# GpSimd's subtraction for the low part of a weight unit in four instructions of 256 columns, not two of 512

## The reference

```python
x = x + 0.5 * swiglu(rmsnorm(x, ffn1_norm), ffn1_w_gu, ffn1_w_down)     # 1024 -> 2 x 2816 -> 1024
x = x + token_mixing(rmsnorm(x, mix_norm), w_in, ...)                   # 1024 -> 3584 -> 1024
x = x + cross_attention(rmsnorm(x, xa_norm), rmsnorm(mem, mem_norm), xa_wq, xa_wkv, xa_wo)
x = x + 0.5 * swiglu(rmsnorm(x, ffn2_norm), ffn2_w_gu, ffn2_w_down)
return rmsnorm(x, final_norm)
```

## Time and profile before

| | before |
|---|---|
| median of 3 runs | 1172.21 us (1170.49 to 1172.48) |
| the profiled execution's own time | 1170.22 us |
| its span, first to last instruction | 1168.4 us |
| TensorE busy | 1141.2 us, 98% |
| TensorE weight load | 948.6 us, 81% |
| DVE busy | 471.4 us, 40% |
| ScalarE busy | 429.2 us, 37% |
| GpSimd busy | 560.1 us, 48%, all but 0.2 in 408 instructions of line 341 |
| DMA | 113.1 MB, mean 97 GB/s |

### The profile page before, as it was taken

The page is one execution under the profiler, slowest core; times in us unless marked ns, Lnnn a source line. Parts: engine busy times, 40 slices in busy tenths (PEclk is TensorE's granted clock), DMA queues, the critical chain, the costliest instruction groups (busy, mean ns, idle before and its releaser), DMA issues.

```text
span 1168.4 us, 14941 instructions
## 1 busy us (share of the span) xinstructions
PE 1141.2 (98%) x5366; PEld 948.6 (81%) x5366; DVE 471.4 (40%) x660; ACT 429.2 (37%) x576; POOL 560.1 (48%) x412
## 2 busy tenths in 40 slices
PE   7999999999999999999999999999999999999997
PEld 4888888888888788888777888888888888888886
DVE  8332233222222568788567224455322322321112
ACT  6332232232223545554346543345223223222221
POOL 5544554555555333233435873145445445455550
PEclk9999999999999999999999999999999999999999
DMA  6323222323223221221222542123232232233312
GB/s 231 106 91 107 96 90 101 103 91 106 99 104 108 90 72 55 73 73 54 82 91 87 182 157 71 53 72 109 90 108 90 90 108 90 90 108 108 108 55 72
DMA packets 33317, 113.10 MB, mean 97 GB/s; under 512 B 3712, under 2 KB 5888, under 8 KB 33152
## 3 DMA queue, kind: packets, MB, share of 16 engines
q1 hardware_dynamic: 33136, 111.53, 27.5%
q10 hardware_dynamic: 144, 1.05, 0.2%
HBM read 110.47 MB, written 2.10 MB: 96 GB/s over the span
## 4 chain that ended last, share of the span: by engine, by line
issue 39%; PE 33%; POOL 27%; POOLq 0%; DVE 0%; ACT 0%; DVEq 0%
POOL wl L341 27%; PE bank L967 11%; PE bank L965 11%; PE bank L966 11%; DVE x L957 0%; POOLq L339 0%; POOLq L337 0%; PE n_bank L1008 0%; PE o_bank L1094 0%; ACT rstd L591 0%; PE o_bank L1095 0%; DVE x L952 0%; PE n_bank L1094 0%; PE n_bank L1095 0%; ACT rstd L592 0%
## 5 line engine op out<-in xcount | busy, mean ns | idle before, releaser
L341 POOL TENSOR_TENSOR wl<-raw,wh 128x512 fp32r<-128x512 f32 x408 | 559.9, 1395 | 582.1 <-ACT wh L353 305.9
L965 PE MATMUL bank<-xh,wh 128*128 128x512 f32 x952 | 375.2, 394 | 0.0
L967 PE MATMUL bank<-xh,wl 128*128 128x512 f32 x952 | 370.8, 389 | 0.0
L966 PE MATMUL bank<-xl,wh 128*128 128x512 f32 x952 | 370.5, 389 | 0.0
L366 ACT ACTIVATE wh<-raw 128x1024 fp32r<-128x1024 f32 x104 | 110.3, 1061 | 396.1 <-DVE ubuf L679 219.4
L966 PEld LDWEIGHTS bank<-xl,wh 128*128 128x128 f32 x952 | 178.8, 188 | 38.3 <-issue 1.7
L965 PEld LDWEIGHTS bank<-xh,wh 128*128 128x128 f32 x952 | 178.7, 188 | 38.2 <-issue 1.7
L967 PEld LDWEIGHTS bank<-xh,wl 128*128 128x128 f32 x952 | 178.7, 188 | 37.7
L353 ACT ACTIVATE wh<-raw 128x1024 fp32r<-128x1024 f32 x99 | 104.3, 1054 | 139.1 <-PE bank L967 137.9
L965 PE MATMUL bank<-hid_h,wh 128*128 128x512 f32 (+1 forms) x374 | 141.0, 377 | 0.0
L967 PE MATMUL bank<-hid_h,wl 128*128 128x512 f32 (+1 forms) x374 | 140.8, 377 | 0.0
(11 more groups left out here) (209 smaller groups left out, 1066.3 us busy)
## 6 DMA issues: line engine op xcount, KB each, us to landing
raw<-w_all SPq DMA_DIRECT2D x204, 512.0 KB, 3.2
x<-x_t SPq DMA_DIRECT2D x8, 256.0 KB, 4.3
out_t<-x SPq DMA_DIRECT2D x8, 256.0 KB, 2.3
memf<-mem_t ACTq DMA_DIRECT2D x1, 1024.0 KB, 4.9
gbuf<-masks_d SPq DMA_DIRECT2D x1, 256.0 KB, 7.9
ident<-ident_d SPq DMA_DIRECT2D x1, 64.0 KB, 7.4
par<-params SPq DMA_DIRECT2D x1, 36.5 KB, 3.1
```

The source lines that it names most:

```text
L341: ins = nc.gpsimd.tensor_tensor(wl[:, c, half], raw[:, c, half], wh[:, c, half].bitcast(f32), SUB)
L965: nc.tensor.matmul(out_, a[0], b_[0], start=first, stop=False)
L966: nc.tensor.matmul(out_, a[0], b_[1], start=False, stop=False)
L967: return nc.tensor.matmul(out_, a[1], b_[0], start=False, stop=last)
```

## The change

In GpSimd's loop over the units, each unit's subtraction is cut into four instructions of 256 columns, in place of two of 512. The semaphore is raised with the last of them, as before. Nothing else is touched: TensorE still waits for the whole unit.

```diff
@@ -337,8 +337,9 @@
             with pool.Fori(0, NU // SLOTS) as i:
                 for c in range(SLOTS):
                     pool.wait_ge(hi_ready, i * SLOTS + (c + 1))
-                    for half in (slice(0, UNIT // 2), slice(UNIT // 2, UNIT)):
-                        ins = nc.gpsimd.tensor_tensor(wl[:, c, half], raw[:, c, half], wh[:, c, half].bitcast(f32), SUB)
+                    for k in range(0, KC, 2):
+                        two = slice(128 * k, 128 * k + 256)
+                        ins = nc.gpsimd.tensor_tensor(wl[:, c, two], raw[:, c, two], wh[:, c, two].bitcast(f32), SUB)
                     ins.then_inc(lo_ready, 1)
```

## The result

The changed kernel takes **1164.89 us** (median of six runs, 1164.72 to 1165.27), the kernel before beside it 1172.17 (six runs, 1170.49 to 1172.49): ratio 0.9941, 95% interval [0.993, 0.9952]. The profiled execution took 1164.72, its span is 1162.9.

The account below looks back on a forecast made before the run. TensorE was taken to bound the kernel. The terms -2.03 - 0.43 + 0.70 + 1.29 + 0 - 0.8 + 0.79 gave -0.5 us: 1169.7 for the profiled run, 1171.7 on the median's scale, range 1168.2 to 1175.0.

Parts of the forecast that it names:

- What bounds the kernel, and where a GpSimd instruction shows: TensorE bounds it; GpSimd's price counts only where TensorE waits for a low part or for VectorE, never in FFN loops.
- the sum: Place-by-place total of all exposed changes in TensorE's waits: -0.5 us; everything else was taken as hidden.
- The piece: A 256-column GpSimd instruction takes 0.71 us, so an undisturbed unit takes 2.84 + 0.04, 0.34 us more than before.
- no fixed cost on GpSimd: Rival: a piece takes 0.625 us, half of the 512-column instruction; total -3.9, 1168.3 us; chance 0.2.
- Units 99, 100, 101, 104 to 109, 132: Unit 99 +1.29, unit 100 +1.01, unit 101 -1.02, units 104 to 109 -0.8, unit 132 +0.79 us.
- the start: VectorE's eight additions of squares end before TensorE is free, so its wait for the sum goes: -2.03 us.
- the end of the first FFN: The last addition ends before TensorE is free, so its wait there goes: -0.43 us.
- K^T: Units from 104: earlier conversion, then GpSimd sets the pace at 3.74 us a unit; -0.8 us in all.
- The cover of unit 1: Unit 1's low part ends at 17.20, its first matmul is at 17.60; just fits up to 0.74 us a piece.
- The mix stage: TensorE's four waits for VectorE chains grow by 0.12, 0.12, 0.34 and 0.12: together +0.70 us.
- The clock: TensorE stretches at 1.2 GHz: 0 in the total; each costs at most 1.75 us, in either direction.
- The 0.22 for "faster": Chance of a gain over 0.2%: 0.17 from the rival without fixed cost, 0.05 from the prediction's own case.

## Why the prediction was wrong

- **What bounds the kernel, and where a GpSimd instruction shows: right.** No unit of the two FFN loops moved. The ledger has steps only at places that the sum names, and at unit 73.
- **The piece: right.** 2.83 us for four undisturbed, 2.84 + 0.04 forecast. With 2.54 for two of 512, 3.40 for eight of 128 and 2.39 for one of 1024, an instruction takes 0.15 us and 2.15 ns a column, to within 0.01 us at all four widths. So the rival "no fixed cost on GpSimd" falls, though its 1168.3 was the nearest number. The rule of the Trainium skill (Advanced Engine Details and Errata, The Read-Write Bubble) that stood behind that rival exempts GpSimd from one kind of cost between instructions; whatever it means, these rows have a fixed cost per GpSimd instruction, and the measurement decides. The Trainium skill's 4497 ns for 2048 columns (GPSIMD Engine Reference, section 3.1) agrees: by the two numbers above it would be 0.15 + 4.40 = 4.55, an estimate that no run here shows.
- **Units 99, 100, 101, 104 to 109, 132, the start, the end of the first FFN: right**, within 0.15 but for the start (-2.53 and -2.07 in two profiles, -2.03 forecast; the sum's own part is -2.1 in both) and K^T (-1.13 for -0.8). The 3.74 a unit forecast for K^T is 3.71. With two pieces there, the losses at 99, 100 and 132 vanish, as they should; but unit 100's comes back behind it, 0.76 at unit 101 and 0.61 at unit 104, which the sum did not have. The cover of unit 1 that "just fits" holds in one profile of the changed kernel; in the other TensorE waits 0.15 us for it.
- **The mix stage: the step that failed.** "Before, two of four differences of the decay (L736, L737) crossed POOL's two instructions and two ran free ... Now all four cross", +0.12 at each of the first two waits and at the fourth. That was read off at the first wait, 399.87, and there all four do cross, in 3.34 us after 3.36 before (3.76 and 3.64 were forecast); the step is -0.14 for +0.12. For the others I took it over, and only looked at the chain directly ahead of the wait. But the chain starts one step earlier, and there the two free differences run ahead of GpSimd's low part and stay free with shorter pieces; only the two that cross are shortened, by 0.55 each. At unit 92 the same pair is at 535.7 to 538.7. -1.1 and -1.0 in place of +0.12 twice: 2.3 us, and with the first and the third wait all 2.4 of this row. Units 81 and 92 alone give these two steps (-1.10, -1.07), and without these two units they are absent. Shown by both.
- **The clock: the larger step.** "Such a stretch costs at most half of itself, 1.75 us, in either direction." The size is right (1.6 to 1.7 measured), the symmetry is not, and the sum had the clock at 0. It also took the 2.0 between the profiled run of before and its median over to the changed kernel unchanged, where 0.2 is left of it; by the two profiles of before, 2.1 apart, that distance is mostly one stretch that costs. The stretches stand behind TensorE's longer waits, and what this change does to VectorE makes those shorter: from 1.87 to nothing at the start, 0.92 to nothing at 461.64, 1.63 to 0.65 at 556.88, 1.79 to 0.26 at 633.54. With two and three stretches in the two profiles of before there was something to give back and little to lose: the effect to expect had one sign (an argument, which no run tests by itself). The one at 633.54 gave nothing back, since TensorE would have waited there anyway; the others did. Roughly: the steps without the clock give -3.9 (the ledger's -5.53 and the 1.59 of unit 73), the median fell by 7.3, and 3.4 is two stretches of 1.7; the second profile of before, which lies in the median's group, has two that cost, 3.2 us of the 7.64 between it and the changed kernel's. That a stretch makes such a step is shown by the two profiles of the unchanged kernel, which differ by little else (0.6 us of a wait at the start); that it makes the groups is borne out by runs at equal steps and different mean clocks (1163.0 and 1164.7 with units 99 and 132 in two pieces; 1167 and 1170 to 1171.5 without 81 and 92). How many stretches the median run has is an estimate from one profile. Why the clock falls after a given wait in one run and not in another stays open: with the same wait at 399.87 it did in the first profile of before and not in the second.
- **The range.** With the two failed steps, the center should have been 5 to 6 us lower. The 0.22 for "faster" was right in kind only for a wrong reason: it was given to the absence of a fixed cost.

## What to carry to other kernels

When an engine that shares something with another is cut into smaller pieces, follow each chain of the other engine back to where it starts, past the instruction just ahead of the wait; two such places held half of this gain. Choose the width by place: shorter pieces where VectorE's chain is what TensorE waits for, longer ones where the low part itself is late, and not so short that the other engine is no longer let in. And when a change shortens an engine's longest waits, count what TensorE's clock gives back, with that sign, and compare with the median of many runs and not with one profile.

## What the runs showed that I had not expected

- At 128 columns a piece is issued every 0.42 us, and one VectorE instruction stood for 6.80 us beside 15 of them; at 256 columns (every 0.70 us) none waited for more than two. The Trainium skill (SBUF — State Buffer, SBUF: two separate sides) has the pair of ports as a lock held for a whole instruction. These rows agree, and they add that the one that waits isn't always the next to get it. What decides there was not tried.
- A wait of TensorE of 0.9 to 1.8 us was followed by 3.4 us at 1.2 GHz in some profiles and not in others with the same wait (1.3 at 399.87 and 1.6 at 556.88 in the two of before; 0.9 at 461.64 before, without, and at 459.94 with all units but 81 and 92 in four pieces, with; 1.8 at unit 104, with in both of before, without where units 68 to 95 alone are in four pieces), and the times of before lie in groups (1170.6, 1172.2, 1173.35). The length of the wait does not decide it: the one of 1.3 us before the scores of the cross attention, at 744.26 before, is in all fourteen profiles, and no stretch follows it in any. Whether a kernel with fewer such waits spreads less isn't shown: 0.4 us in four runs with units 99, 100 and 132 in two pieces, but 1.9 in five with 104 to 107 too.
